# Start bytes of TensorE's operands: residual tiles in rows of 640 columns, other tiles moved by 128 bytes

## What is computed

```
# first block, 512 positions
u = rmsnorm(x, g_mix);  z = u @ w_in                       # 1024 -> 7,440 columns
y = three branches of z (gated linear attention, convolution, sliding window attention)
h = x + (gate0 * y_gla @ w_gla_o + gate1 * y_conv @ w_conv_o + gate2 * y_swa @ w_swa_o) @ w_o
u = rmsnorm(h, g_ffn)
h = h + (silu(conv(u @ w_up)[:2816]) * conv(u @ w_up)[2816:]) @ w_down
# second block, 16 more positions (meta tokens) in front: 528
u = rmsnorm(h, norm1);  proj = u @ w_in_2                  # 1024 -> 6,672 columns
v = [hgrn2 heads of proj, mamba2 heads of proj];  h = h + v @ w_out_2
u = rmsnorm(h, norm2);  h = h + (silu(..) * ..) @ w_down_2 # as above, same widths
out = rmsnorm(h, final)[16:]
```

## Time and profile before

| | |
|---|---|
| median of three runs | 1782.94 us |
| span of the profiled execution, first to last instruction | 1782.0 us |
| TensorE (PE) busy | 1751.7 us, 98% |
| weight loads (PEld) | 1528.3 us, 86% |
| VectorE (DVE) | 1172.7 us, 66% |
| ScalarE (ACT) | 717.4 us, 40% |
| DMA, mean | 86 GB/s |

### The profile page before, as it was taken

One profiled execution on the slowest core, in us unless ns is written; L12 is line 12 of the kernel. 1 busy time (PEld: TensorE's weight loads), 2 busy tenths in 40 slices (PEclk: granted clock), 3 DMA queues, 4 the chain that ended last, 5 costly groups with the idle time before them and its releaser, 6 DMA issues.

```text
span 1782.0 us, 27315 instructions
## 1 busy us (share of the span) xinstructions
PE 1751.7 (98%) x11006; PEld 1528.3 (86%) x11006; DVE 1172.7 (66%) x1808; ACT 717.4 (40%) x1100; POOL 11.8 (1%) x12
## 2 busy tenths in 40 slices
PE   8999999999999999999999999999998999999997
PEld 5777777778878888888899999999988999999885
DVE  5666656655567777744476766788797877777332
ACT  6334433332343333333445454544454533333221
POOL 0000000000000000000000000000000000000000
PEclk9999999999999999999999999999999999999999
DMA  6222222223222323333222122222212233223321
GB/s 200 71 79 75 83 83 81 85 83 95 91 87 95 95 95 95 95 106 95 73 85 73 69 63 71 70 72 72 72 64 68 83 95 95 92 88 95 106 95 59
DMA packets 44540, 153.77 MB, mean 86 GB/s; under 512 B 6000, under 2 KB 6384, under 8 KB 44416
## 3 DMA queue, kind: packets, MB, share of 16 engines
q1 hardware_dynamic: 44416, 152.04, 27.4%
HBM read 149.93 MB, written 2.10 MB: 85 GB/s over the span
## 4 chain that ended last, share of the span: by engine, by line
PE 83%; DVE 10%; ACT 3%; DVEq 1%; issue 1%; ACTq 1%; DMA 0%; POOL 0%; SPq 0%
PE ps L647 81%; DVE arena L1358 3%; ACT arena L978 2%; PE ps L651 2%; DVEq L1897 1%; DVE arena L1365 1%; DVE w_lo L1355 1%; ACTq L1338 1%; ACT w_hi L978 1%; DVE h_res L1355 1%; DVE arena L1355 0%; DVE u_lo L1565 0%; ACT L983 0%; DVE arena L1372 0%; DVE r_bc L1355 0%
## 5 line engine op out<-in xcount | busy, mean ns | idle before, releaser
L647 PE MATMUL ps<-u_hi,w_hi 128*128 128x258 f32 (+3 forms) x2376 | 645.6, 325 | 8.2 <-DVE u_lo L1565 6.3
L647 PE MATMUL ps<-u_hi,w_lo 128*128 128x258 f32 (+3 forms) x2376 | 640.4, 323 | 0.0
L647 PE MATMUL ps<-u_lo,w_hi 128*128 128x258 f32 (+3 forms) x2376 | 637.1, 321 | 0.0
L1355 DVE TENSOR_TENSOR w_lo<-w_raw,w_hi 128x1024 fp32r<-128x1024 f32 (+1 forms) x280 | 341.5, 1220 | 153.1 <-ACT w_hi L978 141.3
L647 PEld LDWEIGHTS ps<-u_hi,w_hi 128*128 128x128 f32 (+1 forms) x2376 | 392.8, 188 | 52.7 <-issue 11.9
L647 PEld LDWEIGHTS ps<-u_lo,w_hi 128*128 128x128 f32 (+1 forms) x2376 | 393.8, 188 | 36.7 <-issue 1.1
L647 PEld LDWEIGHTS ps<-u_hi,w_lo 128*128 128x128 f32 (+1 forms) x2376 | 392.6, 187 | 36.6 <-issue 1.6
L978 ACT ACTIVATE w_hi<-w_raw 128x1024 fp32r<-128x1024 f32 (+1 forms) x280 | 293.9, 1050 | 306.7 <-PE ps L647 299.7
L1365 DVE SCALAR_TENSOR_TENSOR ffn<-full,par,ffn 128x512 f32<-128x512 f32 (+2 forms) x176 | 132.3, 751 | 81.5 <-ACT ffn L978 78.3
L978 ACT ACTIVATE arena<-arena 128x528 f32<-128x528 f32 (+11 forms) x189 | 96.2, 531 | 219.5 <-DVE arena L1358 87.1
L978 ACT ACTIVATE ffn<-full,par 128x512 f32<-128x512 f32 x88 | 67.8, 770 | 274.0 <-DVE full L1358 274.0
(11 more groups left out here) (157 smaller groups left out, 1506.0 us busy)
## 6 DMA issues: line engine op xcount, KB each, us to landing
w_raw<-weights SPq DMA_DIRECT2D x279, 512.0 KB, 3.6
h_res<-xT SPq DMA_DIRECT2D x8, 256.0 KB, 4.7
outT<-h_res SPq DMA_DIRECT2D x6, 256.0 KB, 2.4
cst<-consts SPq DMA_DIRECT2D x1, 730.0 KB, 8.7
outT<-ffn SPq DMA_DIRECT2D x2, 256.0 KB, 2.7
seg<-consts SPq DMA_DIRECT2D x1, 256.0 KB, 8.7
par<-params SPq DMA_DIRECT2D x1, 240.0 KB, 6.2
msk<-cmask SPq DMA_DIRECT2D x1, 128.0 KB, 8.9
```

Source lines behind the costliest of these rows:

```text
L647: return nc.tensor.matmul(out, lhsT, rhs, start=start, stop=stop)
L1355: return V.tensor_tensor(out, a, b, op)
```

## The change

Nothing is added, removed or put in another order. The rows of `u_hi` and `u_lo` become 640 columns long (2,560 bytes, five times 512), and `u_columns` shifts the columns that are used: in all four uses the row, or for the 514 columns of `up2` the row from its first column on, starts at 128 modulo 512. `v_hi` and `v_lo` get such rows too. `cut_of` puts the cut at 256 columns, so that the second half starts at the same byte modulo 512; for `hg` and `mz`, which read the 514 columns in the place of the 528, it is at 242, and only the second half starts at 128 (the first at 184). A tile of 128 bytes, `between`, in front of `w_hi` moves `w_hi`, `w_lo` and all that lies behind, `y`, `m`, `a` and `v` among it, from 128 to 256 modulo 512. The scratch of the software DMA queue is made smaller to have the room; the kernel issues no DMA from there.

```diff
-    return first if n <= BANK else first + BANK - halves(n)[0][1]
+    return first if n <= BANK else first + BANK - cut_of(g)
-def halves(n):
-    half = 2 * -(-n // 4)
-    return [(0, n)] if n <= BANK else [(0, half), (half, n)]
+LINE = 128
+def cut_of(g):
+    return 2 * LINE - USED if GROUPS[g][0] in ("hg", "mz") else 2 * LINE
+def halves(n, cut=2 * LINE):
+    return [(0, n)] if n <= BANK else [(0, cut), (cut, n)]
+U_WIDE = 5 * LINE
+U_SHIFT = {"g_mix": LINE - META, "g_ffn": LINE - META, "norm1": 0, "norm2": -USED}
+def u_columns(which, c0, c1):
+    return slice(c0 + U_SHIFT[which], c1 + U_SHIFT[which])
...
-        u_hi = sb("u_hi", [P, KD, T2], F32R)
-        u_lo = sb("u_lo", [P, KD, T2], F32R)
+        u_hi = sb("u_hi", [P, KD, U_WIDE], F32R)
+        u_lo = sb("u_lo", [P, KD, U_WIDE], F32R)
         w_raw = sb("w_raw", [P, RAW, PER * UNIT])
+        sb("between", [P, LINE // 4])
...
-        v_hi = sb("v_hi", [P, KD, T2], F32R, s3)
-        v_lo = sb("v_lo", [P, KD, T2], F32R, s3)
+        v_hi = sb("v_hi", [P, KD, U_WIDE], F32R, s3)[:, :, 0:T2 - USED]
+        v_lo = sb("v_lo", [P, KD, U_WIDE], F32R, s3)[:, :, 0:T2 - USED]
...
-                        hi, lo = u_hi[:, i, c0:c1], u_lo[:, i, c0:c1]
+                        hi, lo = u_hi[:, i, u_columns(which, c0, c1)], u_lo[:, i, u_columns(which, c0, c1)]
...
-                    cuts = halves(c1 - c0)
+                    cuts = halves(c1 - c0, cut_of(g))
```

More of the change, by code:

```diff
@@ L576, in square_parts @@
                 return g_osq, y_hi[:, n, :], y_lo[:, n, :]
-            return h_osq[:, USED:], v_hi[:, n - GLA_H, USED:], v_lo[:, n - GLA_H, USED:]
+            return h_osq[:, USED:], v_hi[:, n - GLA_H, :], v_lo[:, n - GLA_H, :]
         def main(v):
@@ L690, in group @@
                     else:
-                        hi, lo = v_hi[:, i, c0:c1], v_lo[:, i, c0:c1]
+                        hi, lo = v_hi[:, i, c0 - USED:c1 - USED], v_lo[:, i, c0 - USED:c1 - USED]
                         pe.wait_ge(tile_lo, TILE_NO[("v" if kind == "oh" else "v2", i)])
                     wh, wl = w_hi[:, s % SPL, w:w + rows], w_lo[:, s % SPL, w:w + rows]
-                    cuts = halves(c1 - c0)
+                    cuts = halves(c1 - c0, cut_of(g))
                     for j, (wt, x) in enumerate(((wh, hi), (wl, hi), (wh, lo))):
@@ L705, in ga @@
                 for k in range(KD):
-                    hi, lo = u_hi[:, k, META:T2], u_lo[:, k, META:T2]
+                    at = u_columns("g_mix", META, T2)
+                    hi, lo = u_hi[:, k, at], u_lo[:, k, at]
                     cols = slice(GLA_RANK * k, GLA_RANK * (k + 1))
@@ L1096, in raw @@
                 c0, c1 = norm_columns(which)
-                f(u_hi[:, k, c0:c1], h_res[:, k, c0:c1], ACT.Identity, scale=gain_of(which, k)).then_inc(u_hi_ok, 1)
+                f(u_hi[:, k, u_columns(which, c0, c1)], h_res[:, k, c0:c1], ACT.Identity, scale=gain_of(which, k)).then_inc(u_hi_ok, 1)
             def raw_meta(_):
@@ L1320, in ssm_v2 @@
                 act.wait_ge(S["gated"], t + 1)
-                f(v_hi[:, t, USED:], m_y[:, t, USED:], ACT.Identity, scale=pc("m2norm", t)).then_inc(S["v2hi"], 1)
+                f(v_hi[:, t, :], m_y[:, t, USED:], ACT.Identity, scale=pc("m2norm", t)).then_inc(S["v2hi"], 1)
             def ssm_sum(g):
@@ L1564, in raw @@
                 dve.wait_ge(u_hi_ok, KD * i + k + 1)
-                V.scalar_tensor_tensor(out=u_lo[:, k, c0:c1], in0=h_res[:, k, c0:c1], scalar=gain_of(which, k),
-                                       in1=u_hi[:, k, c0:c1], op0=ALU.mult, op1=ALU.subtract).then_inc(u_lo_ok, 1)
+                at = u_columns(which, c0, c1)
+                V.scalar_tensor_tensor(out=u_lo[:, k, at], in0=h_res[:, k, c0:c1], scalar=gain_of(which, k),
+                                       in1=u_hi[:, k, at], op0=ALU.mult, op1=ALU.subtract).then_inc(u_lo_ok, 1)
             def raw_meta(_):
@@ L1770, in head_v @@
                     h_o[:, USED:], h_or[:, USED:], h_gate[:, i % 2, USED:])
-                hi, lo = (y_hi[:, i, :], y_lo[:, i, :]) if gla else (v_hi[:, i, USED:], v_lo[:, i, USED:])
+                hi, lo = (y_hi[:, i, :], y_lo[:, i, :]) if gla else (v_hi[:, i, :], v_lo[:, i, :])
                 link(V.scalar_tensor_tensor(out=o, in0=o, scalar=pc("gla_norm" if gla else "hg_norm", i), in1=r,
@@ L1886, in ssm_v2 @@
                 dve.wait_ge(S["v2hi"], t + 1)
-                V.scalar_tensor_tensor(out=v_lo[:, t, USED:], in0=m_y[:, t, USED:], scalar=pc("m2norm", t), in1=v_hi[:, t, USED:],
+                V.scalar_tensor_tensor(out=v_lo[:, t, :], in0=m_y[:, t, USED:], scalar=pc("m2norm", t), in1=v_hi[:, t, :],
                                        op0=ALU.mult, op1=ALU.subtract).then_inc(tile_lo, 1)
@@ L1978 @@
     arrays = lay_out({k: np.asarray(v) for k, v in inputs.items()})
-    nc = bacc.Bacc("TRN2", target_bir_lowering=False, num_devices=1)
+    nc = bacc.Bacc("TRN2", target_bir_lowering=False, num_devices=1, dynamic_dma_scratch_size=1024)
     args = [nc.dram_tensor(k, v.shape, mybir.dt.from_np(v.dtype), kind="ExternalInput").ap()
```

## The result

The changed kernel takes 1790.66 us, the median of 19 runs, against 1784.1 us for the kernel before, also 19 runs: a ratio of 1.0032, 95% interval 1.0024 to 1.004. It is slower, by 6.6 us; 1766.4 us was forecast, and the range ended at 1790. The 19 runs of after aren't one cluster: 4 lie at 1784.0 to 1784.8 us, 15 at 1789.6 to 1793.3. The profiled execution took 1784.75 us (span 1782.6 us), so it is one of the four.

The account below looks back on a forecast made before the run. The prediction took TensorE's pace to bound the kernel: 12.2 + 1.0 + 3.6 + 2.4 - 1.2 = 18.0 us less; with 1 us and 0.5 us given back, 16.5 us, so 1766.4 us. The range went from 1748 to 1790.

Parts of the forecast that it names:

- TensorE's pace bounds the kernel, and only it can move the time: Whole kernel: TensorE busy 98% of the span, largest wait 6.3 us, so time is the number of products times their pace.
- The pace depends on where the moving row starts: Products of 512 columns: 231.7 ns in `up` with drifting rows, 226.7 in `down` with rows all at 128 modulo 512.
- Every stretch then settles at the best pace that its shape shows now: All stretches with equal row starts; largest term 816 units of `u`, 231.7 to 226.7 ns a product, 12.2 us less.
- 514 and 528 columns, 3.6 and 2.4 us less: 608 units of 514 columns gain 6 ns each, 296 units of 528 gain 8 ns each, by settling at their best.
- 242 + 272, 1.2 us more: New cut of the 128 units of `hg` and `mz`: a narrow half may not be cheaper; between 0 and 2.6 us more.
- `a` and `m` go together and cost 0: 1,248 products whose rows and weights both move from 128 to 256, distance unchanged: 0, worst end 6.2 us more.
- `y` 1.0 us less: 96 units of `y`, 288 products, from 230 to 226.7 ns, since nothing unsettles them.
- 1.5 us given back: Part of the gain lost: 1 us in the state space part, 0.5 us in the heads of both blocks.
- distance decides, and it gets worse: Rival, 0.22: row against weights counts; `u` at distance 128 settles at its worst, 7.2 us more, 1790 us.
- Place itself: Rival, 0.14: byte 128 modulo 256 is good for a moving row, 256 bad; 7.7 us less, 1775 us.
- nothing changes: Rival, 0.14: another thing in its stage makes `u` slower, or gains and losses cancel; 1783 us.
- further: Rival, 0.08: conflicts cost more than any row shows; 2.6 ns off 7,104 instructions with `u`, 18.5 us on top, 1748 us.

Follow-up runs that it names:

- faster execution: The changed kernel's first profiled execution, one of the four runs at 1784.0 to 1784.8 us; it took 1784.75 us.
- slower cluster: The fifteen of the changed kernel's 19 runs at 1789.6 to 1793.3 us; units are from a second profiled execution, 1789.76 us.
- table of cuts: Settled units from a bench of TensorE alone: weights at 128, eight distances in steps of 32, ten ways to cut; 512 columns take 680 ns at distance 0.
- kernel by the table: Changed kernel without the 128 bytes, 528 columns cut 264 + 264, `v` and `up2` at distance 192 cut 264 + 250: 1766.46 us, ratio 0.9902.
- bench of pairs: TensorE alone, stretches of 24 units for each pair of row and weight start bytes: 680.0 ns a unit at distance 0, 696.6 to 700.0 at 128.
- version at 256: Changed kernel with the 128 bytes in front of `u_hi` instead of the weights, so everything starts at 256 modulo 512: 1775.95 us, ratio 0.9958.
- version with only the rest moved: Changed kernel with the 128 bytes behind `w_lo`: `u` at distance 0, `y`, `m`, `a` and `v` at 128: 1784.8 us, ratio 1.0003.

## Why the prediction was wrong

- *TensorE's pace bounds the kernel, and only it can move the time*: right. Waits, clock and the chain's shares stayed, and the units' times explain the median (+6.4 of 6.6 us in the slower pattern).
- *The pace depends on where the moving row starts*: half right. It does, but only against the weights. `a` at 226.7 ns stood at 128 with its weights at 128; I named both facts and took equal start bytes from unit to unit for the cause.
- *"Every stretch then settles at the best pace that its shape shows now"*: this is the step that failed. The stretches did settle, in the bench within 3 to 7 units. But what a stretch settles at depends on the distance, and the change takes `u` to distance 128, where a unit of `up` keeps 697.1 to 700.0 ns and not 680. Of the 12.2 us forecast for 816 units the change brought none and lost 1.3 (2.2 in the faster execution); in the version without the 128 bytes the units gained 15.0 and 15.5 ns, 12.5 us by the counts.
- *514 and 528 columns, 3.6 and 2.4 us less*: wrong at the change's distance (+3.5 and +1.7 us in the slower cluster), and the working was wrong in kind too. The 10 ns steps in the earlier trace rows are units in drift, not settled paces; the table of cuts couldn't be read off them. The same goes for "that the cut is at 256 and not 264 changes no sum of columns": at distance 0 the 528 columns settle at 731.6 ns with 256 + 272 and at 720.3 with 264 + 264, which is 3.3 us.
- *242 + 272, 1.2 us more*: measured 0.8 us less (717.2 to 710.9 ns).
- *`a` and `m` go together and cost 0*: right, 680.1 and 680.1; and *`y` 1.0 us less*: 0.1.
- *1.5 us given back*: there was no gain to give back here. Where the gain came, in the kernel by the table, it was 4.5 us.
- *The rival "distance decides, and it gets worse"* forecast 1790 us and had 0.22. It was right in its mechanism, in its signs of recognition (0.70, 0.74, `down` unchanged) and in its point of decision (a unit of `up` over 0.697 us: 697.1 to 700.0). Its terms were less so: it took 3.7 us for the 528 columns (1.7), 1.6 for the whole rows (1.3), 2.4 for the 514 columns of `u` and 1.2 for the halves of 242 (3.1 for both together, `up2` being +3.9), and 1.7 of gain in `v` and `y`, where 0.3 were lost. Its sum of 7.2 us met the 6.4 by luck, because errors of up to 2 us cancelled, and because `up2` took the slower pattern: in the faster one it gains 1.8 us, and the kernel stays near 1784. What I held against it, that a steady pattern finds its own distance, is refuted by the bench of pairs.
- *Place itself* (1775 us) falls with the bench of pairs and the version at 256; *nothing changes* comes close only in the four faster runs; *further* has no unit under 680 ns to show with 4-byte products.
- The rule of the Trainium skill, page "SBUF — State Buffer", section "Who interferes with whom", by which TensorE has two independent read ports and never waits on anyone, was set aside by the prediction. Two independent reads wouldn't depend on their distance; for 4-byte tiles they do (680.0 to 703 ns), for bf16 they don't (647.5 at all four).

Two things stay open. Which read meets the moving row's isn't shown: that the distance to the weights counts, and that narrower loads shrink its effect from 23 to 11 ns, points to the weight load, but a load of a quarter the width didn't lower the mean. And what picks one of the two patterns isn't known beyond this: it is set when TensorE starts again after a disturbance, and both times that this fell together with a clock of 0.50 (`up2` of the faster execution, `v` of the version with only the rest moved) the 710 ns pattern followed. That pattern came without such a drop too, so the clock alone isn't the answer.

## What to carry to other kernels

Where TensorE runs 4-byte products with a load each back to back, lay the moving rows at the same byte modulo 256 as the weights (15 to 20 ns in 700 here), and don't move one of the two without the other. For products cut in halves measure cut and distance together on a bench of TensorE alone: its settled units came back in the kernels within some 2 ns (720.0 and 700.0 as 720.3 and 700.1, 740.0 as 738.2). The benefit in a whole kernel is small, 1.0% here, and a part of it is lost where TensorE waits for others. When two things coincide in the fast case (place and distance), the forecast has to be worked out under each before one is chosen.

## What the runs showed of the hardware

- A stream of 4-byte products with 128 weight columns has a settled pace set by the distance of its operands' start bytes modulo 256, 226.7 to 234.3 ns a product of 512 columns (unit 680 to 703), whatever the row length (2,048 or 2,560 bytes), the PSUM bank or the adding.
- A few units after a disturbance it settles; with halves it can settle in either of two patterns for the same instructions, 710 and 726.7 ns a unit, and stay there through a stage of 250 us. The two profiled executions of the changed kernel differ by 5.0 us that way.
- With 32 weight columns in place of 128 the distance counts for 11 ns a unit and not 23, at nearly the same mean (694.8 and 695.9 ns).
- The same stream in bf16 runs at 215.8 ns whatever the distance, 4.8% less time than the best 4-byte one.
- Two halves can cost 700 ns a unit (264 + 250 columns, distance 192) or 733 (258 + 256, distance 128, in one of its two patterns), with the same 514 columns. The worst of the bench, 250 + 264 at distance 128 passed backwards, took 750.
